# A sixth expert slot, an earlier fetch of the first place's output weights, and rewritten norm chains in a three-block transformer kernel

## The chip, the cores and the metric

One core of one Trainium2 chip runs the whole program in one launch. The metric is the device time of that launch in microseconds (us), the median of several executions.

## The reference

Three transformer blocks follow one another on 256 tokens of width 1024, all in float32. Only the first block and the start of the second bear on the change.

```python
def first_block(x, c, ...):
    mod = silu(c) @ w_ada + b_ada
    sh1, sc1, gt1, sh2, sc2, gt2 = split(mod, 6)
    h = rms_norm(x, g_pre_mix) * (1 + sc1) + sh1
    y = hybrid_mixer(h, ...)                       # ends with ... @ w_out
    x = x + gt1 * rms_norm(y, g_post_mix)
    h = rms_norm(x, g_pre_ffn) * (1 + sc2) + sh2
    y = moe_ffn(h, ...)                            # 32 experts, 4 of them for each token
    return x + gt2 * rms_norm(y, g_post_ffn)

# in moe_ffn, for each expert: u = xb @ w_mlp1[e] (1024 x 2048) + b1; gated unit; a @ w_mlp2[e] (1024 x 1024) + b2

def second_block(x, p, ...):
    z = rmsnorm(x, norm_mix_gain) @ w_in ; three token mixers ; x = x + y @ w_out
    x = x + conv_ffn(rmsnorm(x, norm_ffn_gain), ...)
    x = x + sigmoid(x @ ple_w_gate) * (p @ ple_w_proj)
    return rmsnorm(x, final_norm_gain)
```

The third block (two gated FFNs, a gated MLP mixer, a sparse attention) is untouched.

## The kernel before

Each engine runs its own instruction list, and semaphores join them. Dense weights come through a ring of four tiles of 1 MB (`ring`, issued by the sync engine's queue in `loads_sp`, L374). ScalarE copies each tile to a rounded half `hi` (L356), VectorE subtracts to get `lo` (L365), and TensorE multiplies with both.

**The expert stage.** The 32 experts are ordered at run time into 32 places by how many tokens they have. Places 8 and 20 are wide (two groups of up to 64 tokens), places 1, 2, 9, 10, 15, 21, 22 and 31 are thin (32 tokens), the rest take one group of 64. A place needs six loads of 2 MB: four chunks of `w_mlp1` (up, numbered by `up_load(p, c)`) and two of `w_mlp2` (down, `down_load(p, i)`). Expert 0 is always at place 0; the other places' experts are known only when VectorE has written `idx`. The loads go to the tile `expert`, which has NEXP = 5 slots and lies over `ring`, `hi` and `lo` (slots 0 and 1 are the ring). Load number m uses slot m % 5 and waits until load m - 5 has been used up (`expert_free(m - NEXP)`). Loads are numbered and issued in the order: up of place p, then down of place p - 1 (L2224 and L2231, in `experts_sp`). TensorE takes them in the same order (`experts_pe`): in its iteration p it does the up products of place p (L1987, thin ones L1982), the bias (L2005), then the down products of place p - 1 (L2070, thin L2066). Between the up chunks it selects and turns token rows for the next place and scatters the results of place p - 2.

Two waits stand ahead of the first expert load: that the last dense unit's `lo` half is written, and that TensorE has used that unit (L2211). After the expert stage `program_sp` waits until every load that used slots 0 or 1 has been consumed, and then loads four ring tiles of the second block's `w_in`.

**The norm chains.** `xa` holds the residual rows, 128 tokens on the partitions, two row halves b and two column halves h (four "quarters" of 128x512). For a norm (`rms_act`, `rms_dve`) ScalarE squares and sums the two quarters of b = 0 (L507), VectorE adds the sums (L520), ScalarE takes the root (L513), VectorE inverts (L526), ScalarE writes the scaled rows `unit` of b = 0 (L541), then the same for b = 1, where VectorE writes `unit` (L558). TensorE turns the rows (L461, `turn_rows_pe`), and ScalarE (`upper_act`, L476 or L478) and VectorE (`lower_dve`) write the inputs of the next products. Before that, at the ends of the mixer ("post1") and of the experts ("post2"), a normed sum is added to `xa` by `add_normed_act` and `add_normed_dve` (L575 scales, L583 adds). An engine meets the others (`meet`) before the next norm, named "pre2" or "mix2", starts. Norms "pre1", "ffn2" and "fin2" have no such addition in front, though "fin2" follows the gate sum of L2821 and L2825 in `conv_ffn_dve`. `scrap` is the same memory as `x`.

Of the kernel before, what the change touches and what calls it, by code (L numbers as in the profile page):

```python
# [15 lines left out]
DM = 1024  # L16
# [138 lines left out]
class Plan:  # L155
# [162 lines left out]

    def expert_slot(self, m):
        return self.t["expert"][:, m % NEXP, :]  # L320

    def expert_landed(self, m):
        return self.sem(f"expert_in{m % NEXP}"), 16 * (m // NEXP + 1)
# [128 lines left out]
def turn_rows_pe(k, e, nm, src="unit", done=None):  # L452

    banks = [k.bank(e, nm, "turn", i) for i in range(4)]
    for b in range(2):
        for i, bank in enumerate(banks):
            if i % 2 == 0:
                e.wait_ge(*(done or k.dve if b else done or k.act)(nm, "unit", b, i // 2))
# [70 lines left out]
def rms_act(k, e, nm, each=None):  # L529

    t, mv = k.t, k.t["moments"]
    for b in range(2):
        for h in range(2):
            if each:
                e.wait_ge(*each(b, h))
            squares_act(k, e, nm, quarter(t["xa"], b, h), b, h, quarter(t["unit"], b, h))
        root_act(k, e, nm, b)
        if b == 0:
            e.wait_ge(*k.dve(nm, "shift", 0))
            for h in range(2):  # L540
                e.activation(quarter(t["unit"], 0, h), quarter(t["xa"], 0, h), ACT.Copy, scale=mv[:, 0, 1:2]).then_inc(*k.ACT(nm, "unit", 0, h))  # L541


def rms_dve(k, e, nm, add=None):

    t, mv = k.t, k.t["moments"]
# [6 lines left out]
    inverse_dve(k, e, nm, 0)  # L553
    square_dve(k, e, nm, 1)
    inverse_dve(k, e, nm, 1)
    e.wait_ge(*k.dve())
    for h in range(2):
        e.tensor_scalar(quarter(t["unit"], 1, h), quarter(t["xa"], 1, h), mv[:, 1, 1:2], None, MUL).then_inc(*k.DVE(nm, "unit", 1, h))  # L558


def add_normed_act(k, e, nm, src, done):

    for b in range(2):
# [3 lines left out]
        root_act(k, e, nm, b)  # L567


def add_normed_dve(k, e, nm, src, row, frees=None):  # L570

    t, mv = k.t, k.t["moments"]
    for b, h in quarters():
        e.wait_ge(*k.act(nm, "sq", b, h))
        e.tensor_tensor(quarter(t["unit"], b, h), src(b, h), row[:, h * 512:(h + 1) * 512], MUL).then_inc(*k.DVE(frees=frees and frees(b, h)))  # L575
        if h:
            square_dve(k, e, nm, b)
        if (b, h) == (1, 0):
            inverse_dve(k, e, nm, 0)
    inverse_dve(k, e, nm, 1)  # L580
    e.wait_ge(*k.dve())
    for b, h in quarters():
        e.scalar_tensor_tensor(quarter(t["xa"], b, h), quarter(t["unit"], b, h), mv[:, b, 1:2], quarter(t["xa"], b, h), MUL, ADD).then_inc(*k.DVE(nm, "x", b, h))  # L583
# [438 lines left out]
def first_pe(k, e):  # L1022
# [5 lines left out]
    for i in range(4):  # L1028
# [5 lines left out]
        if i == 2:  # L1034
            turn_rows_pe(k, e, "pre1")
# [3 lines left out]
def first_act(k, e):  # L1039
    e.wait_ge(*k.mm("c"))  # L1040
    e.activation(k.t["sc"], k.got("c")[:, 0:KC], ACT.Tanh, scale=0.5).then_inc(*k.ACT("c"))
    rms_act(k, e, "pre1", lambda b, h: k.total("x_in"))
# [551 lines left out]
def mixer_out_pe(k, e):  # L1594
# [9 lines left out]
    turn_rows_pe(k, e, "pre2")  # L1604
# [8 lines left out]
def mixer_out_act(k, e):  # L1613
# [4 lines left out]
    add_normed_act(k, e, "post1", lambda b, h: k.got("w_out", "acc", b, h)[:, :], sums_done(k, "w_out"))  # L1618
    meet(k, e, ACT_, "post1")
    rms_act(k, e, "pre2")  # L1620
# [3 lines left out]
def mixer_out_dve(k, e):  # L1624
# [4 lines left out]
    add_normed_dve(k, e, "post1", lambda b, h: k.got("w_out", "acc", b, h)[:, :], t["g1"], lambda b, h: ("w_out", "acc", b, h))  # L1629
    meet(k, e, DVE_, "post1")  # L1630
    rms_dve(k, e, "pre2")
# [6 lines left out]
def lay_start(k):  # L1638
# [7 lines left out]
    k.sb("causal", [128, 128], I32)  # L1646
    k.sb("x", [128, KC, 256])
    k.t["scrap"] = flat(k.t["x"]).rearrange("p (b n) -> p b n", b=2)
    for n in ("xa", "unit"):
        k.sb(n, [128, 2, DM])  # L1650
# [557 lines left out]
def experts_sp(k, e):  # L2208

    e.wait_ge(*k.lo_at(k.last_dense))  # L2210
    e.wait_ge(*k.used(k.last_dense))  # L2211
    expert = [0] * NE
    for p in range(NE + 1):
        if p == 1:
            e.wait_ge(*k.dve("idx"))
        if 1 <= p < NE:
            expert[p] = e.value_load(k.t["idx"][0:1, p:p + 1], min_val=0, max_val=NE - 1)
        if p < NE:
            W = k.A["w_mlp1"][0, expert[p]].rearrange("(c p r) n -> p c (r n)", p=128, r=2)
            for c in range(4):  # L2220
                m = k.up_load(p, c)
                if m >= NEXP:
                    e.wait_ge(*k.expert_free(m - NEXP))
                e.dma_start(k.expert_slot(m), W[:, c, :]).then_inc(k.sem(f"expert_in{m % NEXP}"), 16)  # L2224
        if p >= 1:
            W = k.A["w_mlp2"][0, expert[p - 1]].rearrange("(i p r) n -> p i (r n)", p=128, r=4)
            for i in range(2):
                m = k.down_load(p - 1, i)
                if m >= NEXP:
                    e.wait_ge(*k.expert_free(m - NEXP))  # L2230
                e.dma_start(k.expert_slot(m), W[:, i, :]).then_inc(k.sem(f"expert_in{m % NEXP}"), 16)  # L2231
# [26 lines left out]
def overflow_pe(k, e, past):  # L2258
    t, wt, act = k.t, k.wide, k.t["s_act"]
    with e.If(past >= 1):  # L2260
        met(k, e, "experts")
        for x in range(NE):
# [40 lines left out]
def overflow_dve(k, e, past):  # L2303
    t, b1T = k.t, k.t["b1T"]
    with e.If(past >= 1):
        met(k, e, "experts")
        gov = t["gov"]
# [34 lines left out]
def moe_out_act(k, e):  # L2342
    acc = k.t["acc"]
    add_normed_act(k, e, "post2", lambda b, h: quarter(acc, b, h), lambda b, h: k.dve("acc", b, h))
    meet(k, e, ACT_, "post2")


def moe_out_dve(k, e):
    acc = k.t["acc"]
    add_normed_dve(k, e, "post2", lambda b, h: quarter(acc, b, h), k.t["g2"])  # L2350
    meet(k, e, DVE_, "post2")


def lay_moe(k, c):
# [4 lines left out]
    with ExitStack() as ci:  # L2359
# [11 lines left out]
        for i in range(2):  # L2371
            k.t[f"xs{i}"] = flat(k.t["unit"])[:, i * 512:(i + 1) * 512]
# [60 lines left out]
def block2_pe(k, e):  # L2433
    t = k.t
    turn_rows_pe(k, e, "mix2")
# [44 lines left out]
def block2_act(k, e):  # L2480
    t, f = k.t, k.t["z"][:, 9:12, :]
    rms_act(k, e, "mix2")
# [81 lines left out]
def block2_dve(k, e):  # L2564
    t, sm, hl, f = k.t, k.t["hg_sm"], k.V["hg_lower_bounds_2"], k.t["z"][:, 9:12, :]
    e0, lb, om = sm[:, 0:3], sm[:, 3:6], sm[:, 6:9]
    rms_dve(k, e, "mix2")
# [145 lines left out]
def conv_ffn_pe(k, e):  # L2713
# [5 lines left out]
    turn_rows_pe(k, e, "ffn2")  # L2719
# [19 lines left out]
    turn_rows_pe(k, e, "fin2")  # L2739


def conv_ffn_act(k, e):
# [37 lines left out]
    meet(k, e, ACT_, "fin2")  # L2780
    rms_act(k, e, "fin2", lambda b, h: k.dve("fin2", "x", b, h))
    upper_act(k, e, "fin2", k.V["final_norm_gain_2"], None, t["x_hi"])
# [1186 lines left out]
```

## Time and profile before

| | us |
|---|---|
| median of 3 runs | 2771.27 |
| lowest, highest | 2766.71, 2777.74 |
| the profiled execution's own time | 2766.06 |
| its span in the profile | 2764.2 |

The page of the profile gives, for each engine, its busy time as a share of the span, and cuts the span into 40 slices of 69 us, with the rate of the DMA engines in each. In the trace the expert stage stands between 183 and 1157 us, the second block between 1164 and 1594 us, and the third fills the rest. SPq is the sync engine's queue. A row of a timeline gives start, duration, engine, line, operation, and in brackets the idle time of the engine before it and what ended that.

### The profile page before, as it was taken

To read this page: it belongs to the slowest core of one execution; us is meant where nothing else is said; L and a number is where in the kernel's file an instruction comes from. 1 tells how busy PE (TensorE), PEld (TensorE's weight loads), DVE (VectorE), ACT (ScalarE), POOL (GpSimd) and SP (SyncE) were. 2 spreads that over 40 slices of the span, in tenths; PEclk is the share of its full clock that TensorE was granted. 3 is DMA by queue.
4 is the path that set the end of the run, shared out by engine and by line. 5 is a ranking of instruction groups with operands and counts; after the bars stand their busy time and mean duration, and the time that the engine had idled before them with its cause. 6 is when DMAs were issued, how large, how long until landed. Compare 5 with 4: busy or idle time off the path is not lost. (4 is left out here: it accounts for less than half of the span.)

```text
span 2764.2 us, 39373 instructions
## 1 busy us (share of the span) xinstructions
PE 2546.4 (92%) x16728; PEld 1800.6 (65%) x16728; DVE 1334.6 (48%) x1885; ACT 920.8 (33%) x1242; POOL 226.5 (8%) x160
## 2 busy tenths in 40 slices
PE   7978899998999999578899899999999999999998
PEld 6652333332333333167799799899889899897897
DVE  4441222211212212276777665666575665766755
ACT  4431011110111111154455444544444444425443
POOL 2000000000000000000000011154020010102300
PEclk9979999999999999887899999999999999989999
DMA  9668999999999999842265466455466466440452
GB/s 320 237 231 350 427 427 404 428 427 427 427 402 425 427 427 428 349 126 91 92 200 186 167 196 210 153 181 199 167 201 207 156 213 209 146 156 32 167 202 103
DMA packets 248701, 713.71 MB, mean 258 GB/s; under 512 B 12531, under 2 KB 186313, under 8 KB 223622
## 3 DMA queue, kind: packets, MB, share of 16 engines
q1 hardware_dynamic: 237136, 690.26, 65.5%
q10 hardware_dynamic: 9734, 17.02, 1.8%
q0 software_dynamic: 1648, 3.82, 0.5%
q8 instruction: 136, 2.23, 0.3%
q14 instruction: 47, 0.39, 0.0%
HBM read 710.01 MB, written 1.05 MB: 257 GB/s over the span
## 5 line engine op out<-in xcount | busy, mean ns | idle before, releaser
L365 DVE TENSOR_TENSOR lo<-ring,hi 128x2048 fp32r<-128x2048 f32 x251 | 598.9, 2390 | 302.4 <-ACT hi L356 302.3
L356 ACT ACTIVATE hi<-ring 128x2048 fp32r<-128x2048 f32 x251 | 476.5, 1900 | 151.5 <-PE bank L626 115.6
L1987 PE MATMUL bank<-expert,xg 128*64 128x512 f32 x1664 | 394.6, 613 | 42.5 <-DMA expert<-in_w_mlp 41.1
L423 PE MATMUL bank<-x_hi,hi 128*128 128x256 f32 x1568 | 364.8, 278 | 0.0
L423 PE MATMUL bank<-x_lo,hi 128*128 128x256 f32 x1568 | 362.1, 277 | 0.0
L423 PEld LDWEIGHTS bank<-x_hi,hi 128*128 128x128 f32 x1568 | 294.7, 188 | 3.2 <-issue 1.6
L423 PEld LDWEIGHTS bank<-x_lo,hi 128*128 128x128 f32 x1568 | 294.5, 188 | 2.5 <-issue 1.0
L1987 PEld LDWEIGHTS bank<-expert,xg 128*64 128x64 f32 x1664 | 115.7, 139 | 257.1 <-issue 227.2
L2114 DVE TENSOR_TENSOR acc<-bank,acc 128x512 f32<-128x512 f32 x104 | 64.6, 682 | 327.7 <-PE bank L2095 327.7
L428 PE MATMUL bank<-x_hi,lo 128*128 128x256 f32 x1568 | 194.3, 276 | 0.6 <-DVE lo L365 0.6
L2070 PE MATMUL bank<-expert,aT 128*64 128x512 f32 x832 | 186.7, 600 | 5.7 <-DMA expert<-in_w_mlp 4.6
L428 PEld LDWEIGHTS bank<-x_hi,lo 128*128 128x128 f32 x1568 | 185.4, 188 | 0.8 <-DVE lo L365 0.8
L2019 DVE TENSOR_SCALAR sx<-bank 128x256 f32<-128x256 f32 x60 | 25.2, 420 | 293.2 <-PE bank L2005 240.5
L2070 PEld LDWEIGHTS bank<-expert,aT 128*64 128x64 f32 x832 | 58.1, 137 | 133.2 <-issue 117.5
L626 PE MATMUL bank<-hi,act_lo 128*128 128x512 f32 x448 | 142.3, 392 | 0.0
L626 PE MATMUL bank<-hi,act_hi 128*128 128x512 f32 x448 | 142.3, 392 | 0.0
L626 PE MATMUL bank<-lo,act_hi 128*128 128x512 f32 x448 | 117.5, 392 | 0.0
L383 ACT ACTIVATE act_hi<-tmp 128x512 fp32r<-128x512 f32 x56 | 35.4, 632 | 240.7 <-DVE tmp L3061 178.3
L1946 ACT ACTIVATE unit<-bank 128x512 f32<-128x512 f32 (+1 forms) x34 | 18.6, 547 | 268.9 <-PE bank L1921 208.6
L626 PEld LDWEIGHTS bank<-hi,act_lo 128*128 128x128 f32 x448 | 84.2, 188 | 18.4
L626 PEld LDWEIGHTS bank<-lo,act_hi 128*128 128x128 f32 x448 | 84.2, 188 | 18.3
L626 PEld LDWEIGHTS bank<-hi,act_hi 128*128 128x128 f32 x448 | 80.4, 188 | 14.4
(647 smaller groups left out, 3779.5 us busy)
## 6 DMA issues: line engine op xcount, KB each, us to landing
expert<-in_w_mlp SPq DMA_DIRECT2D x192, 2048.0 KB, 18.8
ring<-in_l_ffn_w_in SPq DMA_DIRECT2D x88, 1024.0 KB, 5.0
ring<-in_l_ffn_w_out SPq DMA_DIRECT2D x44, 1024.0 KB, 4.8
ring<-in_w_ada SPq DMA_DIRECT2D x24, 1024.0 KB, 6.9
ring<-in_l_gm_w_in SPq DMA_DIRECT2D x24, 1024.0 KB, 5.2
ring<-in_ffn_w_up SPq DMA_DIRECT2D x22, 1024.0 KB, 5.0
ring<-in_w_in SPq DMA_DIRECT2D x21, 1024.0 KB, 7.1
ring<-in_l_gm_w_out SPq DMA_DIRECT2D x12, 1024.0 KB, 4.8
```

The lines of the kernel that those rows point to most:

```text
L356: e.activation(k.half("hi", u), k.slot(j), ACT.Copy).then_inc(*k.up("hi_done"))
L365: e.tensor_tensor(k.half("lo", u), k.slot(k.units[u][0]), k.half("hi", u).bitcast(F32), SUB).then_inc(*k.up("lo_done"))
L383: e.activation(hi[:, c:n, :], x[:, c:n, :], ACT.Copy).then_inc(*k.ACT(nm, "hi", c // step))
L423: e.matmul(o, l, r, start=fresh, stop=False, skip_group_check=True)
L428: t = e.matmul(o, l, r, start=False, stop=False, skip_group_check=True)
L626: m = e.matmul(acc[b, h][:, :], x[:, c, b * 128:(b + 1) * 128], w[:, c, h * 512:(h + 1) * 512], start=fresh[b, h], stop=False, skip_group_ ...
L1946: e.activation(k.t[f"xs{n % 2}"][:, 0:COLS[n]], k.got("xs", n)[:, 0:COLS[n]], ACT.Copy).then_inc(*k.ACT("xs", n, frees=("xs", n)))
L1987: i = e.matmul(banks[n][j][h * CAP:(h + 1) * CAP, :], x, W[:, (2 * h + j) * 512:(2 * h + j + 1) * 512], start=c == 0, stop=False, skip_gro ...
L2019: e.tensor_scalar(t[f"sx{j}"], bank[:, 0:512:2], 7.0, None, MIN).then_inc(*k.DVE("gate", "x", n, j))
L2070: q = e.matmul(banks[n][h * CAP:(h + 1) * CAP, :], a, W[:, r, h * 512:(h + 1) * 512], start=half + r == 0, stop=half + r == 4, skip_group_ ...
L2114: e.tensor_tensor(av, k.got("back", n, b, h)[:, :], av, ADD).then_inc(*k.DVE(*((*key, b, h) if key else ()), frees=("back", n, b, h)))
```

## The change

It has three parts. First, a tile `expert5` of one slot is laid over `x` and `unit`, which are now neighbours in memory, and slots are fixed: up chunk c of every place goes to slot c, down half i to slot 4 + i (`expert_turn`). The selected rows `xs0` and `xs1` move from `unit` to `g1`, and the branch for overflowing experts, which did not run here, first turns `htok` back into `x`. Second, the sync engine's queue issues up chunks 0 and 1 of place 0 without the wait for TensorE's use of the last dense unit, and both down halves of place 0 before it waits for `idx`; the second of these waits until TensorE has turned the last of `x` ("htok", 1, 1). The ring loads after the stage wait only for up chunk 1 of the last place. Third, the norm chains: `unit` of b = 0 is written by VectorE too, ScalarE runs one tiny `Sqrt` ahead of most chains, VectorE adds b = 0 to `xa` before it scales b = 1, ScalarE squares quarters of the next norm as soon as each is added, and ScalarE's meeting point moves behind them. In "fin2" the gate sum goes row half by row half.

```diff
+    def expert_turn(self, m):
+        for p in range(NE):
+            if 0 <= m - self.up_load(p, 0) < 4:
+                return m - self.up_load(p, 0), p
+            if 0 <= m - self.down_load(p, 0) < 2:
+                return 4 + m - self.down_load(p, 0), p
...
@@ norms
-def rms_act(k, e, nm, each=None):
...
-        if b == 0:
-            e.wait_ge(*k.dve(nm, "shift", 0))
-            for h in range(2):
-                e.activation(quarter(t["unit"], 0, h), quarter(t["xa"], 0, h), ACT.Copy, scale=mv[:, 0, 1:2]).then_inc(*k.ACT(nm, "unit", 0, h))
+def rms_act(k, e, nm, each):
+    e.activation(k.t["warm"], k.cc("ident")[:, 0:1], ACT.Sqrt).then_inc(*k.ACT())
+    rms_squares_act(k, e, nm, each)
...
+def rms_unit_dve(k, e, nm, b):
+    t, mv = k.t, k.t["moments"]
+    inverse_dve(k, e, nm, b)
+    e.wait_ge(*k.dve())
+    for h in range(2):
+        e.tensor_scalar(quarter(t["unit"], b, h), quarter(t["xa"], b, h), mv[:, b, 1:2], None, MUL).then_inc(*k.DVE(nm, "unit", b, h))
...
+def chain_act(k, e, nm, src, done, then):
+    e.activation(k.t["warm"], k.cc("ident")[:, 0:1], ACT.Sqrt).then_inc(*k.ACT())
     for b in range(2):
         for h in range(2):
             e.wait_ge(*done(b, h))
             squares_act(k, e, nm, src(b, h), b, h, quarter(k.t["scrap"], b, h))
         root_act(k, e, nm, b)
+    k.mark("act_done", "meet", nm)
+    rms_squares_act(k, e, then, lambda b, h: k.dve(nm, "x", b, h))
+    met(k, e, nm)
...
+def chain_dve(k, e, nm, src, row, then, frees=None):
...
+    for h in range(2):
+        scaled(0, h)
+    if not frees:
+        scaled(1, 0)
+    square_dve(k, e, nm, 0)
+    add(0)
+    if frees:
+        scaled(1, 0)
+    scaled(1, 1)
+    square_dve(k, e, nm, 1)
+    add(1)
+    meet(k, e, DVE_, nm)
+    square_dve(k, e, then, 0)
+    rms_unit_dve(k, e, then, 0)
+    square_dve(k, e, then, 1)
+    rms_unit_dve(k, e, then, 1)
...
@@ experts_sp
     e.wait_ge(*k.lo_at(k.last_dense))
-    e.wait_ge(*k.used(k.last_dense))
     for p in range(NE + 1):
         if p == 1:
+            expert_down_sp(k, e, 0, 0)
             e.wait_ge(*k.dve("idx"))
...
                 m = k.up_load(p, c)
-                if m >= NEXP:
-                    e.wait_ge(*k.expert_free(m - NEXP))
+                if p:
+                    e.wait_ge(*k.expert_free(k.up_load(p - 1, c)))
+                elif c == NSLOT // 2:
+                    e.wait_ge(*k.used(k.last_dense))
...
+        if p >= 2:
+            expert_down_sp(k, e, p - 1, expert[p - 1])
+def expert_down_sp(k, e, p, x):
+    W = k.A["w_mlp2"][0, x].rearrange("(i p r) n -> p i (r n)", p=128, r=4)
+    for i in range(2):
+        m = k.down_load(p, i)
+        if p:
+            e.wait_ge(*k.expert_free(k.down_load(p - 1, i)))
+        elif i:
+            e.wait_ge(*k.mm("htok", 1, 1))
+        e.dma_start(k.expert_slot(m), W[:, i, :]).then_inc(*k.expert_in(m))
...
@@ conv_ffn_dve
-    for b, h in quarters():
-        e.wait_ge(*k.act("ple", "tanh", b, h))
-        e.wait_ge(*k.act("pp", b, h))
-        e.scalar_tensor_tensor(quarter(t["unit"], b, h), quarter(t["unit"], b, h), 1.0, quarter(t["pp"], b, h), ADD, MUL).then_inc(*k.DVE())
-    e.wait_ge(*k.dve())
-    for b, h in quarters():
-        xa = quarter(t["xa"], b, h)
-        e.tensor_tensor(xa, xa, quarter(t["unit"], b, h), ADD).then_inc(*k.DVE("fin2", "x", b, h))
+    xa, unit = t["xa"], t["unit"]
+    for b in range(2):
+        for h in range(2):
+            e.wait_ge(*k.act("ple", "tanh", b, h))
+            e.wait_ge(*k.act("pp", b, h))
+            e.scalar_tensor_tensor(quarter(unit, b, h), quarter(unit, b, h), 1.0, quarter(t["pp"], b, h), ADD, MUL).then_inc(*k.DVE())
+        e.wait_ge(*k.dve())
+        for h in range(2):
+            e.tensor_tensor(quarter(xa, b, h), quarter(xa, b, h), quarter(unit, b, h), ADD).then_inc(*k.DVE("fin2", "x", b, h))
...
@@ program_sp
-    e.wait_ge(*k.expert_free(max(m for m in range(6 * NE) if 2 * (m % NEXP) < NSLOT)))
+    e.wait_ge(*k.expert_free(k.up_load(NE - 1, NSLOT // 2 - 1)))
```

## Rows read from the trace of the kernel before

**Rows 1.** The page: the DMA rate in each of the 40 slices

```profile
GB/s 320 237 231 350 427 427 404 428 427 427 427 402 425 427 427 428 349 126 91 92 200 186 167 196 210 153 181 199 167 201 207 156 213 209 146 156 32 167 202 103
```

**Rows 2.** Waits of the sync engine's queue, 170 to 1160 us: total, times, longest

```profile
SPq L2211 <- PE bank L626: 36.2, 1, 36.2
SPq L2217 <- DVE keys L1872: 24.8, 1, 24.8
SPq L374 <- PE bank L2066: 23.8, 1, 23.8
```

**Rows 3.** Timeline of the ramp of the expert stage, TensorE and the queue

```profile
211.38 1.32 PE L1987 MATMUL bank<-expert,xg 128*64 128x512 f32 x4 [0.89 <-ACT xg L1953]
...
217.50 0.34 SPq L2224 DMA_DIRECT2D expert<-in_w_mlp  x1
...
232.95 0.33 SPq L2224 DMA_DIRECT2D expert<-in_w_mlp  x1
...
236.83 3.35 SPq L2231 DMA_DIRECT2D expert<-in_w_mlp  x2
```

**Rows 4.** The expert tile's loads, 175 to 300 us: from issue to landing

```profile
DMA to landing us min/median/max: 7.6/17.1/22.2
```

**Rows 5.** Windows: stretch, busy (instructions) of PE, PEld, DVE, ACT, POOL, clock, DMA share, GB/s

```profile
460.00:480.00 20.00, 20.00 (x116) 6.68 (x116) 6.67 (x20) 3.73 (x8) 0.00 (x0) 1.00 0.90 349
800.00:820.00 20.00, 20.00 (x106) 6.85 (x107) 2.48 (x4) 1.32 (x3) 0.00 (x0) 1.00 0.98 403
820.00:840.00 20.00, 20.00 (x118) 6.62 (x116) 6.67 (x20) 3.73 (x8) 0.00 (x0) 1.00 0.89 351
```

**Rows 6.** TensorE's waits for expert loads, 525 to 640 us (first), 240 to 1156 us (second)

```profile
PE bank L1987 <- DMA expert<-in_w_mlp: 9.5, 8, 3.0
...
PE bank L1987 <- DMA expert<-in_w_mlp: 41.1, 37, 3.1
```

**Rows 7.** Timeline of the end of the expert stage, TensorE, and one window of it

```profile
1140.28 8.78 PE L2070 MATMUL bank<-expert,aT 128*64 128x512 f32 x32 [1.90 <-DMA expert<-in_w_mlp]
...
1143.49 5.57 PE L2070 MATMUL bank<-expert,aT 128*64 128x512 f32 x24
...
1154.83 1.93 PE L2066 MATMUL bank<-expert,aT 128*32 128x256 f32 x32 [1.17 <-DMA expert<-in_w_mlp]
...
1140.00:1145.00 5.00, 4.72 (x14) 1.77 (x16) 0.35 (x1) 0.00 (x0) 0.00 (x0) 0.66 1.01 429
```

**Rows 8.** Timeline of the chain post1 and pre2

```profile
184.98 2.74 DVE L583 SCALAR_TENSOR_TENSOR xa<-unit,moments,xa 128x512 f32<-128x512 f32 x4
...
189.67 0.20 ACT L513 ACTIVATE moments<-moments 128x1 f32<-128x1 f32 x1 [0.43 <-DVE moments L520]
...
190.11 1.33 ACT L541 ACTIVATE unit<-xa,moments 128x512 f32<-128x512 f32 x2 [0.23 <-DVE moments L526]
...
193.32 0.88 DVE L558 TENSOR_SCALAR unit<-xa,moments 128x512 f32<-128x512 f32 x2
```

**Rows 9.** Timeline of the chain post2 and mix2

```profile
1163.85 0.63 ACT L507 ACTIVATE x<-acc 128x512 f32<-128x512 f32 x1 [6.57 <-issue]
...
1165.20 1.28 ACT L513 ACT_TABLE_LOAD   x1
...
1166.49 0.20 ACT L513 ACTIVATE moments<-moments 128x1 f32<-128x1 f32 x1
...
1174.12 0.20 ACT L513 ACTIVATE moments<-moments 128x1 f32<-128x1 f32 x1 [0.43 <-DVE moments L520]
...
1177.44 3.69 ACT L356 ACTIVATE hi<-ring 128x2048 fp32r<-128x2048 f32 x2
```

**Rows 10.** Timeline of the chain ffn2

```profile
1367.40 2.04 ACT L2749 ACTIVATE pp<-bank 128x512 f32<-128x512 f32 x4
```

**Rows 11.** Timeline of the chain fin2

```profile
1582.36 2.50 DVE L2825 TENSOR_TENSOR xa<-xa,unit 128x512 f32<-128x512 f32 x4
...
1587.75 0.20 ACT L513 ACTIVATE moments<-moments 128x1 f32<-128x1 f32 x1
```

More of the change, by code:

```diff
@@ L457, in turn_rows_pe @@
             if i % 2 == 0:
-                e.wait_ge(*(done or k.dve if b else done or k.act)(nm, "unit", b, i // 2))
+                e.wait_ge(*(done or (k.dve if b else k.act))(nm, "unit", b, i // 2))
             for j in range(2):
@@ L1034, in first_pe @@
         if i == 2:
-            turn_rows_pe(k, e, "pre1")
+            turn_rows_pe(k, e, "pre1", done=k.dve)
     flip_pe(k, e, 3)
@@ L1603, in mixer_out_pe @@
     meet(k, e, PE_, "post1")
-    turn_rows_pe(k, e, "pre2")
+    turn_rows_pe(k, e, "pre2", done=k.dve)
 def sums_done(k, nm, last=3):
@@ L1646, in lay_start @@
     k.sb("causal", [128, 128], I32)
+    k.sb("xa", [128, 2, DM])
+    with ExitStack() as c:
+        k.sb("expert5", [128, 2 * SLOT], F32, c)
     k.sb("x", [128, KC, 256])
     k.t["scrap"] = flat(k.t["x"]).rearrange("p (b n) -> p b n", b=2)
-    for n in ("xa", "unit"):
-        k.sb(n, [128, 2, DM])
+    k.sb("unit", [128, 2, DM])
     k.sb("moments", [128, 2, 3]), k.sb("quart", [128, 4]), k.sb("warm", [128, 1])
@@ L2261, in overflow_pe @@
         met(k, e, "experts")
+        for i in range(4):
+            for j in range(4):
+                c = 2 * i + j // 2
+                m = e.transpose(k.ps[4 + i][:, j * 128:(j + 1) * 128], t["htok"][:, j % 2, c * 128:(c + 1) * 128], k.cc("ident"))
+            m.then_inc(*k.up("slow_mm_done", "back", i))
+        e.wait_ge(*k.at("slow_dve_done", "back", 3))
         for x in range(NE):
@@ L2306, in overflow_dve @@
         met(k, e, "experts")
+        for i in range(4):
+            e.wait_ge(*k.at("slow_mm_done", "back", i))
+            e.tensor_copy(flat(t["x"][:, 2 * i:2 * i + 2, :]), k.ps[4 + i][:, :]).then_inc(*k.up("slow_dve_done", "back", i))
         gov = t["gov"]
@@ L2434, in block2_pe @@
     t = k.t
-    turn_rows_pe(k, e, "mix2")
+    turn_rows_pe(k, e, "mix2", done=k.dve)
     first_units_pe(k, e, [k.bank(e, "w_in_2", n) for n in range(2)], k.first["w_in_2"], ((), ()), "mix2", t["a2_hi"], t["a2_lo"])
@@ L2718, in conv_ffn_pe @@
     acc_free(k, "ple_proj")
-    turn_rows_pe(k, e, "ffn2")
+    turn_rows_pe(k, e, "ffn2", done=k.dve)
     first_units_pe(k, e, [k.bank(e, "cf", 0, half) for half in range(2)], k.cf_up[0][0], ((), ()), "ffn2", t["f2_hi"], t["f2_lo"])
@@ L2738, in conv_ffn_pe @@
     meet(k, e, PE_, "fin2")
-    turn_rows_pe(k, e, "fin2")
+    turn_rows_pe(k, e, "fin2", done=k.dve)
 def conv_ffn_act(k, e):
```

74 lines of the change are left out of this document (28 added, 46 removed).

## The prediction

> **What bounds the kernel now.** I read the page first, for its slices of DMA rate. From the fourth to the sixteenth slice (200 to 1100 us) the rate stands at 427 to 428 GB/s and dips in three places only [rows 1]; no other stage holds it. The expert stage moves 192 loads of 2.097 MB, each 4.91 us at 427 GB/s, 943 us in all, so it is bound by the loads, and what counts is when the queue has none to move. The waits of the queue come next: three long ones stand at the stage's ends (the last dense unit's use, `idx`, and the consumption of the last down load), and the rest are waits for a slot [rows 2]. Then the timeline of the ramp and windows over the dips, to see which free slot the queue is short of [rows 3, 5], TensorE's own waits [rows 6], and the timeline of the stage's end [rows 7]. Last the four norm chains, in which TensorE stands idle and every instruction is on the path [rows 8 to 11]. In the third block no edit is on the path.
>
> **The ramp of the expert stage.** Place 0's up products begin at 211.38 us, released by ScalarE's copy of the selected rows and by no load [rows 3]. So loading chunks 0 and 1 earlier gains nothing by itself. What decides is how many loads the queue has done when slots start to come free. Before: four up loads, then up 1.0 (place 1, chunk 0) in the fifth slot after `idx`; from there each load waits for a chunk of place 0: the sixth load at 217.50 us, the eighth at 232.95, the ninth at 236.83 [rows 3], and from then on the rate is full. After: six loads (four up, two down) are issued before `idx`, and up 1.0 takes the place of up 1.1 at the same event, so the seventh load goes out at 217.50 and the ninth at 232.95. The queue is one load ahead once it runs continuously: **4.9 us**. The second down half waits for the last turn of `x`, with the wait for `idx` and all later loads queued behind it; but in TensorE's list that turn stands ahead of the product that yields `idx`, for which the queue waited 24.8 us [rows 2], so it costs nothing. Without that cover the loads behind would move by the delay one for one.
>
> **The slots in the middle.** From place 2 on the order of loads is unchanged and each waits for the load six before it, not five. The three dips are the wide places: at full rate the stretches would have moved 20 us of data each, and what they lack is 20 x (427-349)/427 = 3.65, 20 x (427-403)/427 = 1.1 and 20 x (427-351)/427 = 3.6, together **8.3 us** [rows 5]. TensorE is busy through all of each, so it is late with the fifth slot back. One slot more buys a load's worth, 4.9 us, more than either place's hole (3.65 and 4.7), so I take all 8.3; the bounds are 0 (TensorE then sets the time) and 8.3. TensorE must catch up later for the time to be kept: it waited 9.5 us for up chunks in the 115 us behind the first wide place alone, and 41.1 us in the whole stage [rows 6], so it can.
>
> **The end of the stage.** Here the fixed slots bite. Down 31.0 and 31.1 now wait for down 30.0 and 30.1, two loads earlier in the order, where before they waited for up chunks four and five ahead of those. The 16 product records of down 30.0 begin at its landing, 1140.28 us. Eight of them take 3.21 us (the clock was granted at 0.66 on the mean of this window, part of it at 1.2 of 2.4 GHz), and the 24 others 0.232 us each, so the sixteenth ends at 1145.35, 5.1 us after the landing [rows 7]. A load issued then lands 7.6 us later at the least [rows 4], so 12.7 us after that landing instead of two loads' 9.8: **2.9 us lost**. Its bounds are 16 x 0.232 + 7.6 - 9.8 = 1.5 (higher clock throughout) and 16 x 0.40 + 7.6 - 9.8 = 4.2 (lower throughout). The last load keeps the same shift, and the stage's end (1154.83 + 1.93 us) with it.
> [...]
>
> **The ring loads behind it.** They waited 23.8 us for the last down load [rows 2] and now go out behind the last expert load. Before, four loads of 1 MB from 1156.8 us took 9.8 us and were first read at 1177.44, after the chain [rows 9]. So this gains nothing; it would be worth something only if the chain shrank by over 8 us.
>
> **The norm chains.** Three things change in them. (a) ScalarE no longer writes `unit` of b = 0: between the root of b = 0 and the squares of b = 1 stood an inversion and two copies of 1.33 us [rows 8]. They leave ScalarE's list, and VectorE's two scalings (0.88 us) run beside the squares. This takes 1.5 us off each chain with the turn behind it. (b) The squares of the next norm begin as soon as b = 0 is added. Before, ScalarE began only after all four additions (184.98 + 2.74 = 187.72 us), and the next root came at 189.67 [rows 8]. (c) The table load goes ahead of the wait.
> *post1, pre2:* with the table there, I put the inversion of b = 0 at 182.2. VectorE then has two additions and two scalings at 2.74/4 = 0.69 us each, the sum, root and inversion of b = 1 (0.7) and two more additions, so the last is done at 182.2 + 6 x 0.69 + 0.7 = 187.1; the sum and the root follow at 187.4 instead of 189.67. With (a), **3.7 us**, and place 0 starts that much earlier.
> *post2, mix2:* ScalarE's first square came at 1163.85 after 6.57 us in which it waited for nothing shown: the branch for overflow stands there. The warming `Sqrt` goes ahead of the squares but behind that branch, so its load and root (1.28 + 0.20) delay them by 1.5 us and only replace the load that stood at 1165.20. VectorE scales without waiting meanwhile. I get the root of mix2 at 1171.8 instead of 1174.12, the start of the weight split at 1173.8 instead of 1177.44: **3.6 us** [rows 9].
> *ffn2:* no table load was in it, so (a) alone, and ScalarE's copies of `pp`, which stood between it and the turned rows at 1367.40 [rows 10], move along: **1.5 us**.
> *fin2:* the additions end at 1582.36 + 2.50 = 1584.86 either way, but b = 0 is squared by then and the table is loaded, so the root comes at 1585.2 instead of 1587.75 [rows 11]; with (a), **4.0 us**.
> *pre1* lies under the first weights' loads: nothing.
> Bounds of the four together: 12.8, and half of that if handovers between engines eat (b). The table load took 1.28 us and the root began 0.01 us behind it [rows 9]. "ScalarE: Activation LUTs", section "What ACT_TABLE_LOAD costs", in the Trainium skill has a drain of some 1.38 us on top of 1283 ns. By the page post1 and fin2 could gain up to 1.4 us more each; the row shows no drain, so the sum goes by the row.
>
> **The sum.** 3.7 + 4.9 + 8.3 - 2.9 + 3.6 + 1.5 + 4.0 = 23.1 us. The profiled execution took 2766.06 us, so 2743.0; it lies 5.2 us under the median of the runs, 2771.27, so the median becomes 2748.2.
>
> **The rivals.** *TensorE sets the pace at the wide places.* For: it is busy 20.00 of 20.00 us there [rows 5]. Against: it waits for loads soon after [rows 6]. Gain 14.8, time 2756.5.
> *The chains give half.* A handover or a meeting point keeps (b) from working. For: each chain is a string of waits between two engines, and post2 has a delay with no cause shown. Against: durations and order are all shown. Gain 16.7, time 2754.6.
> *The sixth slot does nothing.* The queue is no further ahead at 232.95 and the holes stay; only the chains act, less the end. Gain 12.8 - 2.9 = 9.9, time 2761.4. Against: the waits for slots are what holds the queue back in rows 3 and 5.
> *Slower: the loads themselves slow down,* with one more of them in flight into memory next to tiles in use. 184 loads are left after the ramp, 903 us; each per cent of rate costs 9 us. It eats the gain at 2.6% and gives slower by 0.5% (13.9 us) at (23.1 + 13.9)/903 = 4.1%, a rate under 410 GB/s; at 5% the time is 2793. Against: the rate is one and the same in ten slices, with however many in flight.
>
> **How the numbers follow.** Forecast 0.70; TensorE's pace 0.10; half chains 0.10; no slot effect 0.07; slower loads 0.03. Some 0.5% (13.9 us) is what a measurement here can tell from no change; faster by more means below 2757.4. That holds for nearly all of the forecast's cases, and for two thirds of the next two, which lie near the line: 0.83. Within 0.5%: 0.14. Slower: 0.03. The runs of before spread from 2766.71 to 2777.74, so a median may lie 5 us off. The low end is the sum with the smaller loss at the end (24.5) less that spread, and 3 us for a clock that falls less often: 2738. The high end reaches over the half chains and the lost holes to the missing slot effect: 2761.
>
> **What would show it.** Six expert loads issued before `idx`, and the queue's ninth load some 3.7 us before 232.95. No slice or window under 425 GB/s around 460 and 820 us. A pause of about 3 us in the DMA near the end of the stage, with waits of the last two down loads on L2070. The table load ahead of the first squares in post1 and fin2, behind the branch in post2. VectorE writing four quarters of `unit`. The stage from the first to the last expert product shorter by 10.3 us. The prediction is wrong if TensorE stays busy throughout with its waits for loads near zero, if the pause at the end exceeds 8 us, or if a root waits for VectorE's meeting point.

## The result and the profile after

The changed kernel takes 2752.25 us (median of 7 runs, 2745.84 to 2758.69) where the kernel before took 2767.48 on the same chip (7 runs, 2765.69 to 2777.74). The ratio is 0.9945, 95% interval 0.9927 to 0.9962: 15.2 us faster. A second measurement of after, later in the study, gave 0.9956 (0.9938 to 0.9974). The forecast was 23.1 us. The direction and the range held; a third of the forecast gain was missing.

The profiled execution of after took 2756.17 us, with a span of 2754.3. First the page's slices of the DMA rate, to lay beside [rows 1]:

```profile
GB/s 322 233 298 338 427 428 427 428 427 428 427 418 428 427 428 427 280 141 77 111 199 193 163 217 201 167 182 184 150 224 210 157 209 204 141 138 47 158 208 94
```

The first dip (404) is gone, the second (402) is a shallow 418, and the sixteenth slice is full. The windows over the dips, after:

```profile
460.00:480.00 20.00, 20.00 (x140) 6.65 (x140) 9.17 (x24) 4.46 (x10) 0.00 (x0) 1.00 1.01 429
800.00:820.00 20.00, 20.00 (x114) 6.47 (x112) 4.04 (x12) 2.36 (x6) 0.00 (x0) 1.00 0.98 405
820.00:840.00 20.00, 20.00 (x140) 6.42 (x138) 7.58 (x21) 3.63 (x8) 0.00 (x0) 1.00 1.00 419
1125.00:1130.00 5.00, 3.72 (x20) 1.26 (x16) 1.60 (x4) 0.42 (x1) 0.00 (x0) 1.00 0.38 161
```

Of the 8.3 us of holes in [rows 5], 20 x (427-405)/427 + 20 x (427-419)/427 = 1.4 us are left. The last window shows a new hole, at the stage's end: 161 GB/s where the queue had always been full, a pause of 5 x (427-161)/427 = 3.1 us. The timeline of that end, TensorE and the queue (compare [rows 7]):

```profile
1125.44 3.65 PE L2108 MATMUL bank<-expert,aT 128*64 128x512 f32 x16 [0.37 <-DMA expert<-in_w_mlp]
1130.23 3.65 PE L2108 MATMUL bank<-expert,aT 128*64 128x512 f32 x16 [1.14 <-DMA expert<-in_w_mlp]
...
1137.23 1.93 PE L2104 MATMUL bank<-expert,aT 128*32 128x256 f32 x32 [0.60 <-DVE acc L2152]
1143.73 3.17 PE L2104 MATMUL bank<-expert,aT 128*32 128x256 f32 x32 [4.57 <-DMA expert<-in_w_mlp]
...
1129.26 5.14 SPq L2278 DMA_DIRECT2D expert<-in_w_mlp  x2
1134.51 12.33 SPq L387 DMA_DIRECT2D ring<-in_w_in  x4
```

Down 31.0 goes out only at 1129.26, when the products of down 30.0 are done, and down 31.1 at about 1134.07, when those of 30.1 are. TensorE then waits 4.57 us for the last one, and its 32 products take 3.17 us instead of 1.93. From the first product of down 30.0 to the last of the stage it is 1146.90 - 1125.44 = 21.5 us; before, it was 1156.76 - 1140.28 = 16.5.

Then the chain post2 and mix2, ScalarE, VectorE and GpSimd (compare [rows 9]):

```profile
1154.73 1.28 ACT L582 ACT_TABLE_LOAD   x1 [7.33 <-issue]
1156.02 0.20 ACT L582 ACTIVATE warm<-const 128x1 f32<-128x1 f32 x1
1156.13 0.61 ACT L520 ACTIVATE x<-acc 128x512 f32<-128x512 f32 x1
...
1155.00 1.90 DVE L600 TENSOR_TENSOR unit<-acc,g 128x512 f32<-128x512 f32 x3 [3.73 <-issue]
...
1163.20 2.57 DVE L564 TENSOR_SCALAR unit<-xa,moments 128x512 f32<-128x512 f32 x2
...
1166.51 1.86 DVE L564 TENSOR_SCALAR unit<-xa,moments 128x512 f32<-128x512 f32 x2
...
1162.52 2.02 POOL L769 MEMSET hS<- 128x2304 f32 x1 [1015.87 <-DVE xa L606]
1164.47 1.98 POOL L771 MEMSET hgqe<- 128x768 f32 x2
1166.39 1.69 POOL L771 MEMSET hgke<- 128x768 f32 x2
```

The two scalings of a pair, 0.88 us in [rows 8], take 2.57 and 1.86 us here, under GpSimd's memsets. In pre2 of the same profile, where GpSimd does nothing, a pair still takes 0.88:

```profile
186.47 0.88 DVE L564 TENSOR_SCALAR unit<-xa,moments 128x512 f32<-128x512 f32 x2
```

Going down the path by landmarks, each step between two of them in us (gain of after over before, in the profiled executions):

| step | forecast | measured | from |
|---|---|---|---|
| post1, pre2: first square to up products of place 0 | 3.7 | 3.5 | 32.61 to 29.14 |
| one load ahead, and the wide places | 13.2 | 11.1 | seventh load 3.7 ahead of before's sixth (the same event), last place's up products 14.8 earlier |
| end of the stage | -2.9 | -5.0 | 16.5 to 21.5 |
| post2, mix2: last add of `acc` to block 2 | 3.6 | 1.3 | 20.60 to 19.28 |
| block 2 to the first addition of `xa` ahead of its FFN | 0 | -0.8 | 179.83 to 180.62, mean granted clock 0.81 to 0.80 |
| ffn2: from there to the first product of the FFN | 1.5 | 1.7 | 8.48 to 6.80 |
| fin2: last tanh to first product | 4.0 | 3.9 | 12.56 to 8.70 |
| sum | 23.1 | 15.7 | |

At fin2's first product after is 1593.56 - 1577.40 = 16.2 us ahead. Of the 0.5 us beside the sum, 0.2 are what is left of an earlier start of post1's squares (1.5), and 0.3 stay unplaced: place 0's products began 211.38 - 206.40 = 5.0 us earlier, but the seventh load, which waits for their first chunk, went out only 3.7 earlier, since that chunk ran at a granted clock of 0.59 (before: 0.72) and took 7.42 us instead of 6.12. The third block gives 6.3 us of the 16.2 back in this execution. The timed runs do not agree with that last part (15.2 us); the profiles further down show how much this block scatters.

### The profile page after: what moved, and what is told of

The parts are those of the page before. It is cut to its first block and busy times, and to the rows that moved or that the text cites. A ratio compares the mean times of both kernels' runs of the same rounds, so it can differ in the third digit from the quotient of the medians.

```text
span 2754.3 us, 39374 instructions
## 1 busy us (share of the span) xinstructions
PE 2548.6 (93%) x16728; PEld 1805.5 (66%) x16728; DVE 1344.4 (49%) x1895; ACT 914.3 (33%) x1236; POOL 228.3 (8%) x160
## 5 line engine op out<-in xcount | busy, mean ns | idle before, releaser
L1984 ACT ACTIVATE g<-bank 128x512 f32<-128x512 f32 (+1 forms) x34 | 18.6, 547 | 265.8 <-PE bank L1959 196.1
```

## The experiments

All times are set against the kernel before, run in the same rounds on the same chip.

| kernel | ratio | 95% interval | down 30.0 to the stage's end | last add of `acc` to block 2 |
|---|---|---|---|---|
| before | 1 | | 16.5 | 20.60 |
| after | 0.9945 | 0.9927 to 0.9962 | 21.5 | 19.28 |
| after, once more | 0.9956 | 0.9938 to 0.9974 | 21.5 | 19.27 |
| chains alone | 0.9954 | 0.9939 to 0.9969 | 16.5 | 18.90 |
| slots alone | 0.9977 | 0.9966 to 0.9987 | 20.2 | 21.72 |
| ring loads late | 0.9932 | 0.9914 to 0.9950 | 21.4 | 19.24 |
| plain rotation of six | 0.9924 | 0.9900 to 0.9948 | 16.7 | 19.54 |
| last place in freed slots | 0.9920 | 0.9901 to 0.9938 | 16.5 | 17.93 |
| memsets late | 0.9948 | 0.9928 to 0.9968 | 21.6 | 17.67 |
| table load ahead of the branch | 0.9939 | 0.9918 to 0.9960 | 20.0 | 20.80 |
| no branch | 0.9927 | 0.9900 to 0.9954 | 20.4 | 15.18 |
| rotation, memsets late, early table | 0.9918 | 0.9900 to 0.9936 | 16.6 | 19.00 |
| rotation, memsets late | 0.9914 | 0.9891 to 0.9937 | 16.7 | 17.82 |

**Which half of the change does it: the chains alone, the slots alone.** The first keeps after's norm chains with five slots and before's loads:

```diff
     def expert_turn(self, m):
-        for p in range(NE):
-            if 0 <= m - self.up_load(p, 0) < 4:
-                return m - self.up_load(p, 0), p
...
+        return m % 5, m // 5
```

> The changed kernel's norm chains alone; the expert loads, their five slots, order and waits as before the change. The sum of my readings for the chains is 3.75 + 2.0 + 1.7 + 3.9 = 11.3 us less about 1.5 us of lower TensorE clock, so some 10 us below the kernel before (ratio about 0.9965); the expert part alone would then be worth 5 to 6 us. Rival (the chains' gains are lost again in the DMA-bound expert stage, since the chain in front of it is hidden by loads): only 7 us.

It measured 0.9954, 2752.4 us against 2764.12. The 0.9965 of the theory lies inside the interval, the rival's 7 us (0.9975) outside. The slots alone are before's chains with the whole of after's expert part:

> The norm chains of before with the sixth slot, the new order of loads and the early ring loads of after. Theory A, the parts add along the path: the thin products of the last place start about 11 us earlier than before's 1120.69, the last down product ends 5 to 7 us earlier than 1156.76 (the end of the stage gives 5 of the 11 back), the first product of block 2 comes 5 to 7 us earlier than 1181.64, and the whole is 5 to 7 us faster (ratio 0.9975 to 0.9982). Rival B, the slots' gain is lost again behind the experts (the timed runs of chains_only lie as low as those of after): the landmarks move as in A up to block 2, yet the ratio is 0.999 to 1.001, with block 2 longer by as much. Rival C, the slots carry more than the trace of after shows: ratio under 0.996.

It measured 0.9977, 6.4 us, as theory A has it. Its landmarks are those of theory A once the 2.8 us are taken off by which place 0 began earlier in this execution: the last place's up products begin at 1106.53 (14.2 us earlier than before, less 2.8), and block 2 starts at 1172.28 (9.4 earlier, less 2.8). The last down product is 10.5 earlier, less 2.8, somewhat more than the 5 to 7 expected, since the end of the stage gives 3.7 us back here and not 5. The effects add within their intervals (0.9954 x 0.9977 = 0.9931, after 0.9945 and 0.9956). But after is not told apart from the chains alone: beside the new chains, the timed runs show no gain of the slots as this change has them. They show one once the end of the stage is put right: 0.9924 and 0.9920 below, of which the second has an interval that ends under the chains'. With five slots the chains' lead is partly lost in the stage. Its loads are 3.9 us ahead at 232.95 us, but the last place's up products only 1120.69 - 1118.38 = 2.3. These windows of chains alone show where:

```profile
440.00:460.00 20.00, 20.00 (x104) 6.61 (x100) 2.48 (x4) 0.72 (x2) 0.00 (x0) 1.00 0.98 400
460.00:480.00 20.00, 20.00 (x117) 6.49 (x120) 7.82 (x22) 3.73 (x8) 0.00 (x0) 1.00 0.92 361
800.00:820.00 20.00, 20.00 (x104) 6.67 (x102) 2.48 (x4) 0.91 (x3) 0.00 (x0) 1.00 0.93 374
820.00:840.00 20.00, 20.00 (x120) 6.42 (x120) 8.22 (x23) 3.54 (x8) 0.00 (x0) 1.00 0.91 359
```

They lack 1.3 + 3.1 + 2.5 + 3.2 = 10.1 us of data, against 8.3 before: loads that arrive earlier stand longer before a TensorE that is busy anyway. With the sixth slot most of the lead is kept.

**The end of the stage: late ring loads, plain rotation, freed slots.** Three kernels ask what costs 5.0 us there. The first takes the ring loads away from behind the last expert loads:

```diff
-    e.wait_ge(*k.expert_free(k.up_load(NE - 1, NSLOT // 2 - 1)))
+    e.wait_ge(*k.expert_free(6 * NE - 1))
```

> The changed kernel with the four ring loads of the next block waiting, as before the change, for the last expert load to be used. Theory (the ring loads, queued right behind the last expert load, share the DMA engines with it and make it land 9.66 us after its issue instead of about 7.6): the last load lands 7.6 to 7.8 us after its issue, the last down products end 1.9 us or more sooner, and nothing is lost behind, because the ring tiles are still there before the norm chain ends. Rival (the late landing is the pair of loads sharing the rate with each other, 4.9 us apart): landing unchanged within 0.3 us.

The stretch stays at 21.4 us:

```profile
1122.11 8.80 PE L2108 MATMUL bank<-expert,aT 128*64 128x512 f32 x32 [1.90 <-DMA expert<-in_w_mlp]
...
1140.22 3.25 PE L2104 MATMUL bank<-expert,aT 128*32 128x256 f32 x32 [2.87 <-DMA expert<-in_w_mlp]
...
1127.63 3.79 SPq L2278 DMA_DIRECT2D expert<-in_w_mlp  x2
```

The last load lands where the queue alone puts it: 1127.63 + 7.6 (the least from issue to landing, [rows 4]) + 4.91 for the second load = 1140.1. In the second profile of after, with the ring loads right behind, the same sum gives 1126.77 + 7.6 + 4.91 = 1139.3, and 1139.38 was measured; in the first it gives 1141.8 against 1143.73. So the ring loads cost 0 to 2 us, by the execution, and they are not the cause. The theory fell: the last load, issued at 1131.09, landed 9.1 us later, not 7.6 to 7.8 (after: 9.66, and 9.2 in its second profile). The ratio of 0.9932 lies within the interval of after's first measurement and just outside that of its second.

The second gives all loads of six slots in plain rotation, in the order of before, so each waits for the load six before it:

```diff
+        return m % 6, m // 6
```

> The changed kernel with six slots taken in plain rotation (load m in slot m mod 6, waiting for load m - 6), the loads in the order of the kernel before (place 0's down halves behind place 1's up chunks), the ring loads behind the use of load 187. Theory (only the number of slots counts, and the last place's down loads, paired with the place before, cost the pause at the end): the ramp is the same as in the changed kernel, the ninth load issued at about 229.2 us, the middle of the stage the same, and the pause near 1127 us is gone, so the last down products end about 5 us sooner (1141.9 instead of 1146.9) and the time falls by 4 to 5 us, to 2747. Rival (the early fetch of place 0's output weights is worth a load of its own): the ramp is 4.9 us later and the time is no better than the changed kernel's.

The third keeps everything of after and moves only the last place's two down loads, into slots 0 and 1:

```diff
-                return 4 + m - self.down_load(p, 0), p
+                return (m - self.down_load(p, 0), NE) if p == NE - 1 else (4 + m - self.down_load(p, 0), p)
...
-            e.wait_ge(*k.expert_free(k.down_load(p - 1, i)))
+            e.wait_ge(*k.expert_free(k.up_load(p, i) if p == NE - 1 else k.down_load(p - 1, i)))
```

> After with one change at the last place: its two down loads go into slots 0 and 1, which its up products free first, and the ring loads wait for the last expert load to be used. Theory A, the end of the stage loses its time because the last two loads may be issued only once the two down loads of the place before have been used: now both are issued before 1125, no pause of the DMA there (GB/s over 410 until the last one lands), and from the first product of the down products of the place before to the end of the stage's last down product it is 16 to 17 us, as before (16.5) and with plain rotation (16.7), not 21.5: block 2 starts 4.5 to 5.5 us earlier than in ring_late for the same start of the down products. Ratio about 0.992 to 0.9925. Rival B, the TensorE clock makes it: the stretch stays over 19 us although the loads are there.

Both get the stretch back, to 16.7 and 16.5 us. Plain rotation also answers its rival: the ninth load goes out at 224.68, 22.5 us behind the first product of place 0, as in after (22.8, and 19.6 in its second profile), so the early fetch of place 0's output weights is not worth a load of its own. Of the third:

```profile
1125.80 8.78 PE L2108 MATMUL bank<-expert,aT 128*64 128x512 f32 x32 [1.90 <-DMA expert<-in_w_mlp]
1137.25 1.93 PE L2104 MATMUL bank<-expert,aT 128*32 128x256 f32 x32
1140.34 1.93 PE L2104 MATMUL bank<-expert,aT 128*32 128x256 f32 x32 [1.16 <-DMA expert<-in_w_mlp]
...
1126.00:1130.00 4.00, 4.00 (x12) 1.37 (x10) 0.00 (x0) 0.00 (x0) 0.00 (x0) 0.58 1.01 426
```

The clock falls to 0.58 behind the wait of 1.90 us here too, and the stretch is short all the same: the loads were issued before, so the DMA goes on at 426 GB/s, and the wait ahead of the last products is 1.16 us, as before (1.17), not 4.57. They run at full clock (1.93 us). That settles the cause: down 31.x waiting for down 30.x.

**The chain of post2 and mix2: late memsets.** GpSimd's memsets wait until the norm's last scaling is done:

```diff
         meet(k, e, POOL_, n)
+    e.wait_ge(*k.dve("mix2", "unit", 1, 1))
     decay_pool(k, e, "hg", k.t["hS"])
```

> The changed kernel with GpSimd's five memsets (hS, hgqe, hgke) held until VectorE has written the last quarter of unit for mix2. Theory (the memsets hold the SBUF port that VectorE's scalings of unit need, and made them 2.57 and 1.86 us for two instead of 0.88): both pairs take 0.88 us, and from ScalarE's first instruction of the chain to the first product of the second block it takes about 2.7 us less (13.1 instead of 15.8). Rival (the scalings are slow for another reason, as ScalarE's squares of the same rows): they stay at 2.57 and 1.86 us.

Both pairs of scalings are back at 0.88 us, and from the last add of `acc` to block 2 it is 17.67 us instead of 19.28: 1.6 us. The rest of the expected sum is not there, since ScalarE's split and copy stand ahead of block 2 as well (TensorE's last wait is 1.59 us for `a_hi`). In the timed runs 1.6 us cannot be seen (0.9948).

**The delay with no cause shown: an earlier table load, and no branch.** First the warming `Sqrt` ahead of the branch on the overflow count:

```diff
     k.mark("act_done", "meet", "experts")
+    e.activation(k.t["warm"], k.cc("ident")[:, 0:1], ACT.Sqrt).then_inc(*k.ACT())
     past = over_count(k, e)
```

> After with ScalarE's load of the Sqrt table placed ahead of the branch on the overflow count, behind its last copy of the expert stage, not behind it. Theory A: the 1.3 us table load leaves the path between the last accumulated row and the first product of block 2; ScalarE's first square of post2 starts 1.2 to 1.6 us earlier relative to the last add of acc (3.5 us behind it in after, 1.9 to 2.3 here), and block 2 follows 1.3 to 1.6 us earlier. Rival B: the branch itself holds ScalarE (7.3 us in after), so its first square is as late as before and nothing is gained. The whole: 0 to 1.6 us, within the scatter of the timing.

Theory A fell, and the outcome is rival B's with a load more: ScalarE's first square came 1150.88 - 1145.59 = 5.3 us behind the last add of `acc`, in after 4.9. Its timeline shows three table loads instead of one:

```profile
1141.84 1.28 ACT L2218 ACT_TABLE_LOAD   x1
1143.14 0.20 ACT L2218 ACTIVATE warm<-const 128x1 f32<-128x1 f32 x1
1149.59 1.28 ACT L520 ACT_TABLE_LOAD   x1 [6.25 <-issue]
...
1152.24 1.28 ACT L526 ACT_TABLE_LOAD   x1
```

Behind the branch a table is loaded for the square and then another for the root. What the engine held before the branch no longer counts; I take it that the loads are placed at build time, and that the table behind a branch with code in it is taken as unknown; no run shows this. The stretch to block 2 grew to 20.80 us. The table has to be asked for behind the branch, where the change has it. The second kernel leaves the branch out on all engines, and with it the code for tokens over an expert's capacity, which the inputs here never reach:

```diff
-    e.wait_ge(*k.dve("count"))
-    return e.value_load(k.t["count"][0:1, 0:1], min_val=0, max_val=T)
+    return None
...
-    with e.If(past >= 1):
+    if False:
```

> After without the branch on the overflow count: the count isn't read and the code for tokens over an expert's capacity is left out on all engines (with the inputs here it never runs). Theory A: the stretches behind the expert stage in which ScalarE and VectorE waited for nothing shown (7.33 and 3.73 us in after) are the branch. VectorE then goes on within 0.3 us of the last add of acc, ScalarE's table load and root stand right behind its last copy of the expert stage, its first square comes within 0.5 us of that add (3.5 + 1.5 us in after), and the first product of block 2 comes 14.3 to 15.5 us behind that add, not 19.3. Gain 3.7 to 5 us in the trace. Rival B: the stretches are waits that the profile doesn't name (a meeting point, a bank), and the first square comes 3 us or more behind the add all the same, gain under 1 us.

Theory A holds:

```profile
1147.15 2.48 DVE L2143 TENSOR_TENSOR acc<-bank,acc 128x512 f32<-128x512 f32 x4 [8.91 <-PE bank L2126]
1149.76 1.90 DVE L600 TENSOR_TENSOR unit<-acc,g 128x512 f32<-128x512 f32 x3
...
1145.88 1.28 ACT L582 ACT_TABLE_LOAD   x1
...
1148.47 0.63 ACT L520 ACTIVATE x<-acc 128x512 f32<-128x512 f32 x1 [1.01 <-DVE acc L2143]
```

VectorE goes on 0.1 us behind the last add, ScalarE's table load comes before that add is done, and block 2 starts 15.18 us behind it, 4.1 us sooner than in after. How long the branch holds ScalarE past the last add differs from profile to profile: 2.1 us with freed slots, 2.4 in chains alone, 2.8 before, 3.5 in both profiles of after, 3.9 in slots alone. It is in every one of the stretches to block 2 in the table except that of no branch, and explains their differences of up to 1.6 us between kernels with the same chain, except for 0.7 us in chains alone. In the timed runs leaving out the branch (0.9927) cannot be told from after.

**Together.** Plain rotation, late memsets and the early table load; then the same without the early load:

> Six slots in plain rotation, the loads' order of before, GpSimd's memsets of mix2 held back until the norm's scalings are done, and ScalarE's Sqrt table load ahead of the branch. If the parts add: the 19.9 us of rot6 and 1.5 to 3 us more, about 2741 to 2743 us where before is at 2764 (ratio 0.991 to 0.992). Rival: the clock of TensorE in block 2 falls as block 2 starts earlier, and the ratio stays at rot6's 0.9924.

> Six slots in plain rotation, the order of loads of before, the norm chains of after, GpSimd's memsets of mix2 held back; the table load where after has it. It is best without the early table load, which cost a load more (two loads of 1.28 us behind the branch, not one). Theory: 1.3 us less than best in the trace from the last add of acc to the first product of block 2, a ratio of 0.991 to 0.992. Rival: the extra load lay beside VectorE's work, and nothing changes.

They measured 0.9918 and 0.9914 (2742.33 us where before took 2765.05). Without the early load the stretch to block 2 is 17.82 us instead of 19.00, 1.2 where 1.3 was expected; the timed runs do not tell the two apart. The second has the lowest ratio of the study, 22.7 us under before; its interval ends at 0.9937, where the estimates for after are 0.9945 and 0.9956, though the first of those has an interval that overlaps it.

**The changed kernel once more.**

> The changed kernel once more, unchanged. Theory: TensorE's pace in the last FFN is a matter of the execution, not of the kernel: 32 products of x_lo by hi took 3.93 us in this kernel's first profile and 3.79 in those of before, chains_only, slots_only, last_free and warm_early, at a granted clock of 1.00 in both. It may come out at either; if it is 3.79, the third block is 4 to 6 us shorter at the same code. The ratio comes out at 0.9935 to 0.9955. Rival: 3.79 and 3.93 belong to the kernel's layout, then it is 3.93 again.

The ratio of 0.9956 lies just above what was expected (0.9935 to 0.9955). One row each, of after's first profile and its second:

```profile
2564.29 3.93 PE L634 MATMUL bank<-x_lo,hi 128*128 128x256 f32 x32
```

```profile
2559.90 3.79 PE L634 MATMUL bank<-x_lo,hi 128*128 128x256 f32 x32
```

The same code runs the same products at two paces. The spans of the two executions are 2754.3 and 2745.5 us; from fin2's first product to the end it is 1176.9 and 1173.0, and 1170.6 before. So 3.9 of the 6.3 us that the third block seemed to give back belong to the execution. The other 2.4 us are within the scatter too: the kernel with the late ring loads, whose third block is the same code, took 1167.6 for this stretch, less than before did, and the thirteen profiles lie between 1166.8 and 1176.9. The pace does not explain this: 1167.6 came with 3.93 us, and 1175.1 (chains alone) with 3.79.

## Why the prediction was right, and where its sum was off

**The bound and the ramp: right.** Six loads go out before `idx`, and the ninth goes out at 229.20 us, 3.75 ahead of the 232.95 at which the eighth went before [rows 3]: one load ahead, and the 3.7 us by which the seventh went out sooner. The wait for the last turn of `x`, costed at nothing, was 13.3 us long and ended at 195.92, ahead of `idx`.

**The slots in the middle: mechanism right, size 2.1 too large.** The step that took all 8.3 us of holes failed by 1.4. The holes are gone at the first wide place and smaller at the second, where TensorE stays behind the loads even with six slots (405 and 419 GB/s after, 393 and 428 with plain rotation), so the sign "no slice or window under 425" failed. A hole of 4.7 us was compared with one slot's 4.91 us, which left no room for the lead that the chains and the ramp add; chains alone shows that such a lead deepens the holes. The other 0.7 us I cannot place.

**The end of the stage: mechanism right, forecast 2.9, measured 5.0, above its upper bound of 4.2.** The landing of the last load comes 18.3 us behind the first product of down 30.0 (before: 1154.83 - 1140.28 = 14.6), a loss of 3.7, and 18.1 in the second profile of after, a loss of 3.6. So far the bounds held. The term left out is the products behind the pause: they ran at the lower clock, 3.17 us (3.34 in the second profile) instead of 1.93, another 1.2 to 1.4. The Trainium skill says in "TensorE: Matmul & The Clock Gate", section "Why this matters for your kernels", that long idle gaps between bursts of products bring the clock down; the trace agrees behind the pause of 4.57 us, with 0.78 granted from 1142 to 1146 us. It is no fixed price: with the same waits, slots alone and the early table load show a pause of 2.9 us there and the last products at 1.93, and stretches of 20.2 and 20.0, while late ring loads have the same pause and 3.25.
That the landing comes so near the forecast is in part luck in the first profile. The 5.1 us of products ahead of the issue, costed at partly the lower clock, ran at full clock there (16 in 3.65 us), and down 31.0 went out 3.8 us behind the first of them; the 2.0 us between the queue's own 1141.8 and 1143.73, with down 31.1 issued 4.8 behind it and the ring loads right behind that, made up for it. In the second profile the sum holds as it was meant: issue at 1126.77 - 1121.25 = 5.5 us, and the last load on the same shift. Before the change, down 31.0 and 31.1 waited for the loads five ahead of them, up 31.1 and 31.2, and went out at 1127.73 and 1132.63, 12.6 and 7.7 us ahead of the first product of down 30.0.

**post2 and mix2: forecast 3.6, measured 1.3.** This is the part that fell short most, and its mis-sized term is the scalings, put at 0.88 us a pair from a chain in which GpSimd is idle. An engine that the argument left out becomes free at the meeting point of post2, starts its memsets there, and now meets VectorE's scalings, which before came when it was through. Late memsets show 1.6 us for it. The Trainium skill says in "SBUF — State Buffer", section "SBUF: two separate sides", that GpSimd and VectorE's fast modes share a port pair as an exclusive lock, the loser blocked for the whole instruction. The rows agree with it: 2.57 and 1.86 us beside memsets, 0.88 without, and the memsets of `hgqe`, 1.42 us before, take 1.98. Taken singly the instructions go in turns: each of the four scalings ends 0.28 or 0.29 us behind the end of a memset (1164.81 behind 1164.53, 1165.77 behind 1165.49), and the memsets that start beside one take 1.01 or 1.02 us instead of 0.74. Another 0.7 us is the branch: ScalarE's first instruction came 2.8 us behind the last add of `acc` before and 3.5 after. Together 1.3 + 1.6 + 0.7 = 3.6; but the branch's part varies by more than that between profiles, so only the 1.6 is the change's own for certain.

**post1 and pre2, ffn2, fin2: right** within 0.2 us each. The first root of fin2 came 1573.04 - 1572.56 = 0.48 us behind the last addition (forecast 0.3), the table long there:

```profile
1569.31 1.28 ACT L544 ACT_TABLE_LOAD   x1
...
1571.27 1.29 DVE L2879 TENSOR_TENSOR xa<-xa,unit 128x512 f32<-128x512 f32 x2
...
1573.04 0.20 ACT L526 ACTIVATE moments<-moments 128x1 f32<-128x1 f32 x1 [1.01 <-DVE moments L533]
```

**The rivals.** The sixth slot does something: slots alone is 0.9977, with 1 outside its interval. TensorE's pace at the wide places took 1.4 us, not 8.3. The loads did not slow down: 427 or 428 GB/s in eleven slices (before: in nine, not ten, and the fourth slice, 350, belongs to the ramp). "The chains give half" is wrong in the sum (3.5 + 1.3 + 1.7 + 3.9 = 10.4 of 12.8), though the chain that had the delay with no cause shown did fall short. The measured 15.2 us lie next to the 14.8 of the first rival, and that is chance: its mechanism gave 1.4 of its 8.3 us, and the rest came from the end of the stage and from post2.

**What else did not come out.** The stage from the first to the last expert product was to be 10.3 us shorter; it was 945.4 - 940.5 = 4.9 (7.0 in the second profile): 2.1 are missing in the middle, 2.1 at the end, and 1.3 went to the first chunk of place 0 at the lower clock. The 9.8 us for the four ring loads of the kernel before were worked out from the full rate; in its profile their median from issue to landing is 10.4 us. Nothing in the sum hung on that.

## What to carry to other kernels

When slots are bound to kinds of loads, check the last round: each last load must wait for something freed long before, for else the whole latency from issue to landing stands in the open, and the clock may fall behind the pause. When a chain is made shorter, list every engine that its meeting points release, and see what those will run beside. A branch between two stages costs its own microseconds on each engine, and what was prepared ahead of it (here a table) may be gone behind it.

## What the runs showed of the hardware

- TensorE runs the third block's products at one of two paces, 3.79 or 3.93 us for 32, with the granted clock shown as 1.00 in both. Of thirteen profiles seven have the first and six the second, and the same kernel showed each once. What sets the pace, no run shows; the length of the third block, 1166.8 to 1176.9 us, does not follow it.
- The mean clock granted from 1180 to 1355 us was 0.79 to 0.81 in twelve of thirteen profiles, and 0.88 in that of chains alone, whose block 2 took 180.9 us from its first product to the first of its FFN (after: 187.4, before: 188.3). No run settles whether its timing brought this about or chance.
- A pair of VectorE scalings and a pair of GpSimd memsets slow each other down: 0.88 to 2.57 us for the one, 1.42 to 1.98 for the other.
- An untaken branch on a value in memory shows as a wait for "issue", 5.9 to 7.7 us on ScalarE (part of it beside the last products and additions of the stage) and 2.4 to 4.2 on VectorE, and leaving it out took 4.1 us off the path.
